# Hierarchical scores of the HGRN mixer: the diagonal blocks as 32-wide products on four partition quarters

## The reference, cut to what matters

```python
G = jnp.cumsum(lfc, axis=1)
diff = jnp.where(incl[None, :, :, None, None], G[:, :, None] - G[:, None, :], -jnp.inf)
attn = jnp.einsum('bthk,bshk,btshk->bhts', qc, kc, jnp.exp(diff))
o = jnp.einsum('bthk,bhkv->bthv', qc * jnp.exp(G), S) + jnp.einsum('bhts,bshv->bthv', attn, vc)
```

## Time and profile before

| | us |
|---|---|
| median of 3 runs | 4034.54 (4027.77 to 4037.85) |
| the profiled execution, whole | 4043.51 |
| its span in the trace | 4041.7 |
| TensorE busy | 3454.8 (85%) |
| VectorE busy | 1936.3 (48%) |
| ScalarE busy | 1276.3 (32%) |
| GpSimd busy | 616.3 (15%) |

### The profile page before, as it was taken

How to read it: one execution, slowest core, us unless ns; L and a number is a source line. 1 busy time by engine, 2 the same in 40 slices (tenths; PEclk the granted TensorE clock), 3 DMA queues, 4 the chain that set the end, 5 groups by cost and what they waited for, 6 DMA issues and landing times. The chain is left out here.

```text
span 4041.7 us, 50879 instructions
## 1 busy us (share of the span) xinstructions
PE 3454.8 (85%) x20578; PEld 3140.0 (78%) x20578; DVE 1936.3 (48%) x2606; ACT 1276.3 (32%) x1748; POOL 616.3 (15%) x610
## 2 busy tenths in 40 slices
PE   4699999994577777777738596999999999999998
PEld 3599999994467666666638485999999999999987
DVE  3333322211566667666641575445445444454465
ACT  3333322321222222212210253334334333343354
POOL 0000000000565655555530000000000000000000
PEclk7799999997787888887865798999999999999999
DMA  6322232221121121211110465533444434434453
GB/s 234 139 58 61 61 79 75 85 66 37 74 79 50 67 78 39 78 70 47 45 58 0 151 221 210 212 128 125 172 141 171 144 125 175 141 125 162 141 199 125
DMA packets 224879, 449.50 MB, mean 111 GB/s; under 512 B 41096, under 2 KB 112958, under 8 KB 217502
## 3 DMA queue, kind: packets, MB, share of 16 engines
q1 hardware_dynamic: 223718, 445.11, 32.1%
q10 hardware_dynamic: 976, 1.78, 0.1%
HBM read 363.38 MB, written 83.47 MB: 111 GB/s over the span
## 5 line engine op out<-in xcount | busy, mean ns | idle before, releaser
L2024 PE MATMUL ff_p<-ff_h_hi,ff_w_hi 128*128 128x384 f32 (+1 forms) x1536 | 502.3, 327 | 23.7 <-DMA ff_h_lo<-tmp_h 23.7
L2026 PE MATMUL ff_p<-ff_h_hi,ff_w_lo 128*128 128x384 f32 (+1 forms) x1536 | 502.6, 327 | 0.0
L2025 PE MATMUL ff_p<-ff_h_lo,ff_w_hi 128*128 128x384 f32 (+1 forms) x1536 | 501.7, 327 | 0.0
L435 PE MATMUL pin_pz<-hi,pin_whi 128*128 128x424 f32 (+1 forms) x1320 | 469.4, 356 | 15.6 <-DVE pin_wlo L551 15.6
L436 PE MATMUL pin_pz<-lo,pin_whi 128*128 128x424 f32 (+1 forms) x1320 | 467.0, 354 | 0.0
L437 PE MATMUL pin_pz<-hi,pin_wlo 128*128 128x424 f32 (+1 forms) x1320 | 467.0, 354 | 0.0
L2043 PE MATMUL ff_p<-ff_w_lo,ff_f_hi 128*128 128x512 f32 (+1 forms) x1088 | 426.7, 392 | 0.0
L2044 PE MATMUL ff_p<-ff_w_hi,ff_f_lo 128*128 128x512 f32 (+1 forms) x1088 | 426.4, 392 | 0.0
L2042 PE MATMUL ff_p<-ff_w_hi,ff_f_hi 128*128 128x512 f32 (+1 forms) x1088 | 423.9, 390 | 0.3 <-DVE ff_f_lo L2138 0.3
L2127 DVE TENSOR_TENSOR ff_w_lo<-ff_w,ff_w_hi 128x1024 fp32r<-128x1024 f32 x192 | 235.1, 1225 | 345.4 <-ACT ff_w_hi L2075 345.4
L2075 ACT ACTIVATE ff_w_hi<-ff_w 128x1024 fp32r<-128x1024 f32 x192 | 203.6, 1060 | 388.9 <-PE ff_p L2044 384.4
(11 more groups left out here) (477 smaller groups left out, 5965.6 us busy)
## 6 DMA issues: line engine op xcount, KB each, us to landing
ff_w<-in_w_unit SPq DMA_DIRECT2D x192, 512.0 KB, 3.6
ff_w<-in_w_unit SPq DMA_DIRECT2D x48, 2048.0 KB, 8.0
mix_zt<-tmp_z SPq DMA_DIRECT2D x16, 2176.0 KB, 8.6
tmp_z<-pin_z SPq DMA_DIRECT2D x32, 1024.0 KB
pro_wa<-in_w_ada SPq DMA_DIRECT2D x24, 1024.0 KB, 8.1
mix_rb<-tmp_rows_p SPq DMA_DIRECT2D x16, 1152.0 KB, 11.2
pin_w<-in_w_in SPq DMA_DIRECT2D x33, 512.0 KB, 7.8
tmp_h<-op_h_hi SPq DMA_DIRECT2D x17, 512.0 KB, 3.8
```

The lines of the kernel that those rows point to most:

```text
L435: pe.matmul(pz[:, g, 0:n], whi[:, u, k], hi[:, k, at:at + n], start=(k == 0), stop=False)
L2024: pe.matmul(dst, w1_hi[:, u, k], hi, start=(k == 0), stop=False)
L2025: pe.matmul(dst, w1_hi[:, u, k], lo, start=False, stop=False)
L2026: mm = pe.matmul(dst, w1_lo[:, u, k], hi, start=False, stop=(k == KT - 1))
```

## The change

The eight terms are taken apart by where their pairs lie. The diagonal and the levels n = 1 to 16 (six terms, `NEAR`) have all pairs inside the four diagonal blocks of 32 tokens. Their products are made block by block: keys of 32 tokens (64 x 32 weights) with the queries of the same 32 tokens, into the same quarter of `pd`'s partitions, side by side for the six terms. Both pairs of heads still take a round each, now at levels 2 and 4. VectorE masks 128 x 2 x 192 values by a compact mask `level_c` and, at level 5, sums the six terms by one `tensor_reduce` into `near` (128 x 4 x 32). Levels n = 32 and 64 need no mask: their pairs fill whole blocks off the diagonal, and `far` multiplies just those (32 x 32 and 64 x 64). ScalarE copies the blocks from `pd` and `near` to their places in `ps` (`place`, at level 6), whose other blocks are set to zero once. GpSimd's `add_up` goes. In the sample stage there are levels n = 1, 2, 4 only and no `far`; `far` and `place` stand in `rest` there.

A new function `allowed` holds the waits of `round` and `far` and is called at a level's start, ahead of its first product, where the waits of a round stood just before the round's products.

```diff
-        plan = [("turn", 0), ("turn_before", 0)] + [("round", i) for i in range(len(groups))]
-        fill = [[plan[i]] if i < len(plan) else [] for i in range(halvings)]
-        rest = plan[halvings:] + [("mlstm", 0), ("hgrn", 0)]
-        R = len(groups)
+        plan = [[("turn", 0)], [("turn_before", 0)], [("round", 0)], [], [("round", 1)], [("far", 0), ("near", 0)], [("place", 0)]]
+        fill = plan[:halvings]
+        rest = [step for slot in plan[halvings:] for step in slot] + [("mlstm", 0), ("hgrn", 0)]
+        R = 2
...
+                def allowed(what, i):
+                    if what == "round" and i == 0:
+                        pe.wait_ge(S("hk"), v(2, 2))
+                        pe.wait_ge(S("hq"), v(1, 1))
+                        pe.wait_ge(S("gated"), v(1, 1))
+                    elif what == "round":
+                        pe.wait_ge(S("masked"), v(R, 1))
+                    elif what == "far" and not sample:
+                        pe.wait_ge(S("masked"), v(R, 2))
...
-                        for n in range(4):
+                        j = i
+                        for n in range(NEAR):
+                            for at in diagonal:
+                                for par in range(2):
+                                    if n == 0:
+                                        a, b = z[half(par), R_HG0 + 2 * j + 1, at], z[half(par), R_HQ + j, at]
+                                    else:
+                                        a, b = hk[half(par), n - 1, j, at], hq[half(par), n - 1, j, at]
+                                    mm = pe.matmul(pd[at, par, near_at(j) + n * CB:near_at(j) + (n + 1) * CB], a, b,
+                                                   start=True, stop=True)
+                        mm.then_inc(S("round"), 1)
+                    elif what == "far" and not sample:
+                        for j in range(2):
+                            for s in (0, 2 * CB):
+                                for par in range(2):
+                                    pe.matmul(pd[s:s + CB, par, far32_at(j):far32_at(j) + CB], hk[half(par), BLOCKY, j, s:s + CB],
+                                              hq[half(par), BLOCKY, j, s + CB:s + 2 * CB], start=True, stop=True)
                             for par in range(2):
...
+                                mm = pe.matmul(pd[half(0), par, far64_at(j):far64_at(j) + HD], hk[half(par), BLOCKY + 1, j, half(0)],
+                                               hq[half(par), BLOCKY + 1, j, half(1)], start=True, stop=True)
+                        mm.then_inc(S("far"), 1)
...
-                        pe.wait_ge(S("summed"), v(2, 2))
+                        pe.wait_ge(S("summed"), v(1, 1))
...
                 for l in range(halvings):
+                    for what, i in fill[l]:
+                        allowed(what, i)
...
+                    elif what == "place":
+                        if not sample:
+                            act.wait_ge(S("far"), v(1, 1))
+                            for j in range(2):
+                                for s in (0, 2 * CB):
+                                    act.activation(ps[s:s + CB, j:HH:2, s + CB:s + 2 * CB],
+                                                   pd[s:s + CB, :, far32_at(j):far32_at(j) + CB], ACT.Copy)
+                                act.activation(ps[half(0), j:HH:2, half(1)], pd[half(0), :, far64_at(j):far64_at(j) + HD],
+                                               ACT.Copy)
+                        act.wait_ge(S("near"), v(1, 1))
+                        for at in diagonal:
+                            ins = act.activation(ps[at, :, at], near[at], ACT.Copy)
+                        ins.then_inc(S("summed"), 1)
...
-                    if l >= 4:
-                        add_up(l - 4)
...
-                for i in range(len(groups)) if sample else [3]:
-                    add_up(i)
...
+            dve.memset(ps[:], 0.0)
+            for at in diagonal:
+                dve.tensor_copy(level_c[at], level[at, 0:NEAR, at])
...
-                        dve.tensor_tensor(ph[:, j:HH:2, 4 * g:4 * g + 4, :], pv(pd, P, n=4),
-                                          level[:, 4 * g:4 * g + 4, :].unsqueeze(1).broadcast_to([P, 2, 4, P]),
-                                          ALU.mult).then_inc(S("masked"), 1)
+                        dve.tensor_tensor(ph[:, j:HH:2], pd[:, :, near_at(j):near_at(j) + NEAR * CB].rearrange("p r (n c) -> p r n c", c=CB),
+                                          level_c[:].unsqueeze(1).broadcast_to([P, 2, NEAR, CB]), ALU.mult
+                                          ).then_inc(S("masked"), 1)
+                    elif what == "near":
+                        dve.wait_ge(S("masked"), v(R, 2))
+                        dve.tensor_reduce(near[:], ph[:].rearrange("p h n c -> p h c n"), AX.X, ALU.add).then_inc(S("near"), 1)
```

More of the change, by code:

```diff
@@ L831 @@
 BLOCKY = 5
+CB = 1 << BLOCKY
 Y_M, Y_G, Y_H = 0, MH, MH + GH
@@ L876, in mixers @@
         hk, hq = (sb(n, [P, LEVELS + 1, 2, P]) for n in ("hk", "hq"))
-        ph = sb("ph", [P, HH, LEVELS + 1, P])
+        NEAR = min(halvings, BLOCKY) + 1
+        ph = sb("ph", [P, HH, NEAR, CB])
+        level_c = sb("level_c", [P, NEAR, CB])
+        near = sb("near", [P, HH, CB])
         ps = sb("ps", [P, HH, P])
@@ L894, in mixers @@
         y_out = [S(f"y_out{u}") for u in range(nbuf)]
-        groups = [(j, g) for j in range(2) for g in range((halvings + 1) // 4)]
-        terms = halvings + 1
         MASKED = min(halvings, BLOCKY)
-        plan = [("turn", 0), ("turn_before", 0)] + [("round", i) for i in range(len(groups))]
-        fill = [[plan[i]] if i < len(plan) else [] for i in range(halvings)]
-        rest = plan[halvings:] + [("mlstm", 0), ("hgrn", 0)]
-        R = len(groups)
+        plan = [[("turn", 0)], [("turn_before", 0)], [("round", 0)], [], [("round", 1)], [("far", 0), ("near", 0)], [("place", 0)]]
+        fill = plan[:halvings]
+        rest = [step for slot in plan[halvings:] for step in slot] + [("mlstm", 0), ("hgrn", 0)]
+        R = 2
         CONSTS = 2
+        near_at = lambda j: j * (NEAR * CB + CB + 2 * CB)
+        far32_at = lambda j: near_at(j) + NEAR * CB
+        far64_at = lambda j: 0 if j else far32_at(0) + CB
+        diagonal = [slice(at, at + CB) for at in range(0, P, CB)]
         pv = lambda b, w, at=0, n=3: b[:, :, at:at + n * w].rearrange("p r (j c) -> p r j c", c=w)
@@ L1047, in step @@
                     elif what == "round":
[L1048 to L1054, removed]
-                        for n in range(4):
-                            for par in range(2):
[L1057 to L1062, removed]
@@ L1063, in step @@
-                        mm.then_inc(S("round"), 1)
+                        j = i
[8 more added lines that the diff above has]
+                                                   start=True, stop=True)
@@ L1323, in body @@
                 v = lambda n, c: t * n + c
[L1324 to L1340, removed]
-                        pool.tensor_tensor(ph[:, j:HH:2, 4, :], ph[:, j:HH:2, 4, :], ph[:, j:HH:2, 5, :], ALU.add
-                                           ).then_inc(S("part"), 1)
-                        pool.wait_ge(S("part"), v(R, i + 1))
-                        pool.tensor_tensor(out, out, ph[:, j:HH:2, 4, :], ALU.add).then_inc(S("summed"), 1)
                 pool.wait_ge(S("lt"), v(1, 1))
```

1 line of the change is left out of this document (removed).

## The result

| | before | after |
|---|---|---|
| median, us | 4035.39 (4027.77 to 4037.85) | 4071.99 (4060.69 to 4091.7) |
| ratio | | 1.0096 (95%: 1.0077 to 1.0116) |
| profiled execution, us | 4043.51 | 4060.69 |

Slower by 1%, where 3957 was forecast. The 17 are in the mixer stage: the first tile ends 2.4 us later, the fifteen after it take 63.62 us each instead of 62.73 (13.3 together), and all the rest is 1.5.

What follows compares the result with a forecast made beforehand. No engine was full, so waits decide: TensorE's for GpSimd's last addition and VectorE's before `wn`. Per-tile terms −9, gates +15 and tails −83 sum to −77 us, from median 4034.5 to 3957; own range 3929 to 3985, overall 3928 to 4015.

Steps and rivals of the forecast that it cites:

- The tail: Tile's end: without GpSimd's additions, `wn` starts 7.8 us after X (end of the last `xt` update), −5.5 us a tile.
- The undisturbed chain: VectorE from X (last `xt` update's end) to mLSTM's end: 7.5 us with GpSimd idle, before 0.3 added for `hk`.
- Masks and sum: VectorE: two masks at 0.93 us and a 0.9 us reduce replace four 1.22 us masks; −0.3 a tile, at levels 5 and 6.
- `lx` at clock 1.00: Sign at the tile's end: TensorE's product `lx` would run at full clock, where it had 0.50 after its stall.
- The hoisted waits: Waits ahead of a level's first product: +1.0 us at level 2 (0.7 to 1.3), +0.35 at level 5, per tile.
- The rounds: TensorE's 96-record rounds at levels 2 and 4: 13 ns a record, 1.28 us each; +0.2 and +0.25 a tile.
- rival 1: TensorE's rounds: a record costs 26 ns, a round 2.5 us, +39 us, total 3996; chance 0.17.
- rival 2: TensorE's rounds pace by the record: 52 ns, 5.0 us a round, total 4076, slower; chance 0.10.
- Level 3: Level 3 loses its round, and its next product waits for the `m` copy alone: −0.25 us a tile.
- `cl`: GpSimd's `cl` of level 4 no longer stands behind the first addition, so TensorE waits less: −0.84 us a tile.
- Rival 3: Clock falls to 0.50 in levels 2 to 5 because small products leave the array mostly empty: +2.3 a tile, 3994; chance 0.08.
- rival 4: Tile's end: the stall only moves, to late ScalarE copies or VectorE's chain keeping 8.9 us; −4.4, 3974; chance 0.05.

Runs made afterwards that it cites:

- experiment 2: Changed kernel, with GpSimd's keys of the next tile also waiting until `wn` is made: 3994.26 us, ratio 0.9889 to the kernel before.
- experiment 4: Changed kernel, with VectorE doing mLSTM's end (`den` to `cm`) behind `rv` and not ahead of `wn`: 3989.04 us, ratio 0.9878 to the kernel before.
- experiment 12: Changed kernel, with the six masked terms of a score laid side by side so the sum reads in order: 4059.97 us, ratio 1.0069.
- experiment 1: Changed kernel, with VectorE's sum of the six terms behind level 5's second update, not ahead of it: 4052.58 us, ratio 1.0038.
- experiment 5: Changed kernel, with the sum behind level 5's second update and mLSTM's end behind `rv`: 3944.29 us, ratio 0.9754.
- experiment 6: Changed kernel, with the sum behind level 5's second update and GpSimd's keys waiting for `wn`: 3955.53 us, ratio 0.9787.
- experiment 3: Changed kernel, with the hoisted waits back behind each level's `m1`, on small extra products: 4040.75 us, ratio 1.0009.
- experiment 7: Changed kernel, with the sum and mLSTM's end moved later and level 2's waits back behind `m1`: 3924.86 us, ratio 0.9709.
- experiment 9: On top of experiment 7, `far`'s wait for the second mask also behind level 5's `m1`: 3922.79 us, ratio 0.973.
- experiment 11: On top of experiment 7, the keys of the levels start once `far` has read the old ones: 3910.88 us, ratio 0.9702.
- experiment 10: On top of experiment 7, each round's 48 products issued twice (192 records a round): 4034.83 us, ratio 0.9994.

## Why the prediction was wrong

*The tail, forecast −5.5 a tile, measured −1.9, and +1.3 behind it.* TensorE's wait went, the places are filled in time, `cc` takes 0.17 and `ex` 1.76 as forecast. The step that failed is "the next `hk` starts once HGRN's product is out, about 4 us after X, and disturbs mLSTM's end, for which I add 0.3". Time and place were right (X + 4.9), the price was not: up to 7 us, not 0.3. L1410's 2.69 us, which the prediction read as GpSimd's doing and then took for gone, looks like the same effect: in the tenth tile it runs to 1645.20, and a GpSimd instruction ends at 1645.16, though not the first that it stands beside. So a warning was there to be read: what is held is held at least to the end of a GpSimd instruction, and `hk` has 4.0 us. The undisturbed chain itself was put a little too long: it ends at X + 6.5 in experiment 2's tile, not 7.5, since L1412 and L1417 had been held beside L1410 too. Experiments 2 and 4 take the collision away in two ways and win 2.1 and 2.2% against the changed kernel's ratio.

*Masks and sum, forecast −0.3, measured +0.8 at level 6.* The sum took 1.52 and not 0.9, for its stride (experiment 12), and stood before the update that TensorE waits for. The prediction counted it by its length in a pause that was full, and missed what a stall there does to the clock: "`lx` at clock 1.00" held in five tiles of fifteen. Experiments 1, 5 and 6 show the price of its place. The masks were over-priced: each covers 384 values, 0.55 us, not 0.93.

*The hoisted waits, +1.0 and +0.35*: of the right size for level 2 (1.0 in experiment 3; 1.5 in experiment 7, over the stated 1.3), nothing to be told from none for level 5 (experiment 9).

*The rounds, +0.2 and +0.25*: 1.04 us each, at the lower bound; level 4 (its product to its update) gave −0.07. Rivals 1 and 2 fell with that. *Level 3, −0.25, and `cl`, −0.84*: measured −0.25 and −0.82.

*The rivals.* Rival 3 had the clock fall in the wrong place and by another cause; rival 4 named the pieces ("VectorE's chain keeps its 8.9") but not a chain that gets longer. No rival had the stall go to another pair of engines because TensorE was faster. That a chain shrinks to its undisturbed length assumed that the disturber stays away, though its start hung on the very product that came sooner.

With collision and stall cured the forecast's mechanism gives 3955.5 (experiment 6). That this meets 3957 so closely is in part luck: X to `wn` fell by 6.1 us and not 5.5, `wn` to `lt` by 1.0 and not 0, level 2 rose by 1.8 and not 1.2, and the keys wait for `wn`, which the forecast didn't have. With mLSTM's end moved instead and level 2's waits back it is 3924.9 (experiment 7), 2.9% under the kernel before; experiment 11's version measured lowest, 3910.9, by its ratio not to be told from experiment 7's.

Open: why the clock falls in the middle of HGRN's products in some tiles (`lx` at X + 5.5 to 6.1) even in experiments 5 to 7; which tiles the stall before level 6 costs the clock; 20 of the 35 us of experiment 3; whether the pauses of experiment 10 are the supply of instructions; and what the changed kernel's three untraced executions, up to 31 us longer, had more of.

## What to carry to other kernels

When a wait on the path goes, list what was released by the instruction behind it: all of it comes sooner, and beside other work than before. For GpSimd and VectorE that work is to be read by operands: here VectorE's instructions with two inputs in SBUF, and one small one with a single input, lasted as long as GpSimd's, while those that read PSUM did not. And put a reduction behind, not ahead of, the update that another engine waits for: in six tiles of fifteen a stall of 1.3 us went with half the clock for the 10 us behind it, and no shorter stall did.

## What was not expected of the hardware

Products with 64 x 32 weights on two row halves and four column quarters took 11 ns a record over 96 records (1.04 us), where 64 x 128 weights took 52 ns. Series of 192 of them brought pauses of 2 to 4 us, which look like a lack of instructions. A VectorE sum over a stride of 32 values took 1.52 us for 768 values, 0.95 in order; a mask written with a stride of 6 took 0.84 for 0.55.
